# Block one's opening in a new order: the first half of features through modulation, then keys, filter layers and queries

## The chip, the cores and the metric

One core of one Trainium2 chip runs the whole program. The metric is device time in microseconds of one execution, the median of the runs shown. The engines are named as in the profile: PE is TensorE (PEld its weight loads), DVE is VectorE, ACT is ScalarE, POOL is GpSimd, SP is SyncE, which only issues DMAs here.

## What is computed

Two transformer blocks on 256 tokens of 1024 features. The change touches the start of the first one alone. Everything is float32. Cut to what matters:

```python
mx = (sc @ w_mod[l] + b_mod[l])[:, None, :]          # sc = silu(c)
mc = scc @ w_mod[l] + b_mod[l]                       # scc = silu(c_ctx)
sh1, sc1, g1, sh2, sc2, g2 = jnp.split(mx, 6, axis=-1)
csh1, csc1, cg1, csh2, csc2, cg2 = jnp.split(mc, 6, axis=-1)
hc = modulate(rms_norm(ctx, norm1_g[l]), csh1, csc1)  # h * (1 + scale) + shift
pkv = hc @ w_in[l][:, OFF_K:OFF_HY]                   # keys and values of the context
spec_x = hyena_spectrum(n_lat, hy_f_w1[l], ...)       # a small network with two sine layers
hx = modulate(rms_norm(x, norm1_g[l]), sh1, sc1)
yx, _, _ = mixer_sublayer(hx, kc, vc, rope, w_in[l], ...)   # queries, keys, values, hyena, fourier, gates
x = x + g1 * yx
h2 = modulate(rms_norm(x, norm2_g[l]), sh2, sc2)
x = x + g2 * expert_choice_moe(h2, w_router[l], w_gate[l], w_up[l], w_down[l])
```

Behind it come a final norm and a second block of two layers.

## The kernel before

Each engine has a program of its own, written out by hand in the order in which it runs; counting semaphores join them. `c.xtv`, `c.mod` and the like are such counters, `P.wait_ge(c.mod, 3)` a wait. Every engine executes strictly in its program's order, so a wait holds all that is written behind it.

Loads: the list `queue` is issued by SP in its order (L2867 to L2876). A 1 MB weight tile goes to one of six ring slots, and its DMA waits until the slot's last reader is done. `wmod` is the modulation weight. It has 12 column blocks of 512 columns, each in two loads (the two halves of the 1024 input features). `MODS` gives the order in which the blocks are done: `p` counts places in that order, `n` is the block. Blocks 0 and 1 are the two halves of the shift `sh1`, 2 and 3 those of the scale `sc1`.

One modulation block goes through four steps. `mod_products` on PE multiplies the two conditioning rows with eight weight slices (L506), `mod_evict` copies the sums out of PSUM on DVE or ACT, `mod_turn` on PE turns them into columns with four matmuls (L516), and `mod_add` on DVE adds the bias (L1436). `affA` is (1 + scale) times the norm's gain. Once scale and shift of a half are there, `turned_rows` on DVE and ACT apply them to the turned tokens of x (transposed on PE, L665) and write `XT1`. `high_half` (ACT) and `low_half` (DVE) then split `XT1` into `XTH` and `XTL`, two reduced-precision parts. The first weights are split the same way by `part()`: ACT writes the high part and DVE the low part (L1409). A product of split operands is three matmuls, `mm3` (L488 to L490). `q_half(m, h)` is such a product for the queries: tokens m (128 of them), half h of the features. `keys_values` (L641) multiplies the unsplit `XT1` (or `XT2`, the context) with the unsplit weight `wkv`; its argument `ks` lists the eight slices of 128 features.

The filter network: `filter_in(0)` and `filter_in(1)` are its two layers. A small matmul on PE is followed by a chain of seven DVE operations that reduce the sine's argument, and by ACT's sine. `filter_out` and `filter_sum` follow, `context_rows` turns the context's tokens. `turn_over(b, n)` issues n matmuls of the identity with itself into PSUM bank b; nobody reads them. After the queries and keys, `beside()` spreads the hyena, fourier and gate products between the steps of attention.

## Time and profile before

| what | us |
|---|---|
| median of 3 runs | 2299.32 |
| lowest and highest | 2298.85, 2299.82 |
| the profiled execution | 2296.84 |
| its span | 2295.5 |
| block one up to the first expert products | about 325 |
| expert stage | about 325 to 1219 |

The profiled execution is one run with the hardware profiler; its span is the time from the first to the last instruction. A timeline row is a run of equal instructions: start, busy time, engine, line, operation, written tile, read tiles, shape and count, and in brackets how long the engine had been idle and who ended that. A window row gives, for a stretch, the busy time of each engine, the clock that TensorE was granted (1.00 is full), the share of the 16 DMA engines and what they moved. The chain is followed back from the last instruction, so it names what everything waited for. A matmul of float32 appears as two records, a transpose as one.

### The profile page before, as it was taken

The numbers are of one execution on the slowest core, as the hardware profiler recorded it, in microseconds if no ns is written. First come the engines' busy times: TensorE is split into PE (matmuls) and PEld (weight loads), VectorE is DVE, ScalarE is ACT, GpSimd is POOL, SyncE is SP. The second block draws the span as 40 slices with busy tenths as digits, with TensorE's granted clock in tenths as the row PEclk, the third lists the DMA queues.
The fourth block names the chain that finished last, engine by engine and source line by source line (L and its number), as shares of the span: only waits on it lengthen the run. The fifth ranks groups of instructions, "written<-read, shape, count | busy, mean of one in ns | idle before, by whom it ended". The sixth has DMA issues, their size and how long they took to land.

```text
span 2295.5 us, 28914 instructions
## 1 busy us (share of the span) xinstructions
PE 1927.1 (84%) x12324; PEld 1348.0 (59%) x12324; DVE 982.9 (43%) x1219; ACT 668.9 (29%) x811; POOL 66.8 (3%) x144
## 2 busy tenths in 40 slices
PE   7899998556555566655589999999999999999998
PEld 4777962111111111111137998779998999778997
DVE  4745651000000000000006657875667666876656
ACT  4432420000000000000004444554445444455444
POOL 0000000000000000000001001010000000100000
PEclk9999999887878888787899999999999999999999
DMA  9156899999999999999997564245544555324552
GB/s 373 67 197 233 320 388 429 431 431 431 431 431 429 432 431 431 430 430 433 431 399 282 195 207 157 110 149 188 196 165 175 185 198 181 141 100 168 199 193 85
DMA packets 53489, 647.44 MB, mean 282 GB/s; under 512 B 5936, under 2 KB 6448, under 8 KB 10096
## 3 DMA queue, kind: packets, MB, share of 16 engines
q1 hardware_dynamic: 53360, 645.59, 70.5%
q8 instruction: 97, 1.59, 0.3%
q14 instruction: 32, 0.26, 0.0%
HBM read 644.52 MB, written 1.05 MB: 281 GB/s over the span
## 4 chain that ended last, share of the span: by engine, by line
PE 57%; DMA 32%; DVE 7%; ACT 2%; issue 1%; POOL 0%; SPq 0%; DVEq 0%; ACTq 0%; POOLq 0%
DMA wide_b<-in_experts 29%; PE PS L488 14%; PE PS L490 13%; PE PS L489 13%; PE PS L986 4%; PE PS L951 4%; DMA ring<-in_wgt 1%; DMA ahead<-in_wmod 1%; DVE low L1895 1%; PE PS L929 1%; DVE low L1409 1%; PE PS L641 1%; DVE PS L1920 1%; PE PS L1263 1%; DVE XR L1959 1%
## 5 line engine op out<-in xcount | busy, mean ns | idle before, releaser
L1895 DVE TENSOR_TENSOR low<-ring,WH 128x2048 fp32r<-128x2048 f32 (+1 forms) x163 | 372.1, 2283 | 182.5 <-ACT WH L2284 179.9
L488 PE MATMUL PS<-XH,WH 128*128 128x256 f32 x1408 | 396.9, 282 | 3.4 <-DVE XL L1927 3.3
L489 PE MATMUL PS<-XL,WH 128*128 128x256 f32 x1408 | 395.1, 281 | 0.0
L490 PE MATMUL PS<-XH,low 128*128 128x256 f32 x1408 | 393.1, 279 | 0.0
L2284 ACT ACTIVATE WH<-ring 128x2048 fp32r<-128x2048 f32 (+1 forms) x164 | 313.1, 1909 | 26.9 <-DMA ring<-in_fg 18.9
L488 PEld LDWEIGHTS PS<-XH,WH 128*128 128x128 f32 x1408 | 264.5, 188 | 7.0 <-issue 5.2
L490 PEld LDWEIGHTS PS<-XH,low 128*128 128x128 f32 x1408 | 267.5, 190 | 0.0
L489 PEld LDWEIGHTS PS<-XL,WH 128*128 128x128 f32 x1408 | 264.6, 188 | 1.4
L1877 DVE TENSOR_TENSOR T1S<-T1S,PS 128x512 f32<-128x512 f32 x16 | 11.0, 688 | 536.7 <-PE PS L951 536.7
L951 PE MATMUL PS<-ring,big 128*32 128x512 f32 x936 | 133.8, 721 | 57.9 <-DMA ring<-in_experts 57.9
L2558 ACT ACTIVATE T1S<-PS 128x512 f32<-128x512 f32 x16 | 9.6, 597 | 540.2 <-PE PS L951 540.2
L986 PE MATMUL PS<-wide_b,PBT 128*32 128x512 f32 x480 | 86.6, 886 | 75.2 <-DMA wide_b<-in_experts 75.2
L951 PE MATMUL PS<-wide_a,big 128*32 128x512 f32 x480 | 81.1, 827 | 71.4 <-DMA wide_a<-in_experts 71.3
L488 PE MATMUL PS<-WH,FH 128*128 128x512 f32 x352 | 139.6, 397 | 0.4 <-DVE FL L2025 0.4
L490 PE MATMUL PS<-WH,FL 128*128 128x512 f32 x352 | 138.5, 393 | 0.0
L489 PE MATMUL PS<-low,FH 128*128 128x512 f32 x352 | 138.4, 393 | 0.0
L1885 DVE TENSOR_TENSOR T1S<-PS,ATG 128x512 f32<-128x512 f32 x32 | 22.1, 692 | 262.4 <-PE PS L986 261.8
L951 PE MATMUL PS<-wide_b,big 128*32 128x512 f32 x480 | 77.0, 790 | 56.3 <-DMA wide_b<-in_experts 56.3
L951 PEld LDWEIGHTS PS<-ring,big 128*32 128x32 f32 x936 | 31.9, 128 | 154.6 <-issue 80.7
L488 PE MATMUL PS<-WH,XH 128*128 128x512 f32 (+1 forms) x256 | 104.6, 408 | 4.5 <-DVE low L1895 3.5
L986 PEld LDWEIGHTS PS<-wide_b,PBT 128*32 128x32 f32 x480 | 19.1, 154 | 140.2 <-DMA wide_b<-in_experts 85.8
L490 PE MATMUL PS<-WH,XL 128*128 128x512 f32 (+1 forms) x256 | 99.5, 388 | 0.0
(447 smaller groups left out, 2816.1 us busy)
## 6 DMA issues: line engine op xcount, KB each, us to landing
wide_b<-in_experts SPq DMA_DIRECT2D x30, 4096.0 KB, 23.7
wide_a<-in_experts SPq DMA_DIRECT2D x29, 4096.0 KB, 23.8
ring<-in_experts SPq DMA_DIRECT2D x28, 4096.0 KB, 24.0
ring<-in_fg SPq DMA_DIRECT2D x44, 1024.0 KB, 5.0
ring<-in_fu SPq DMA_DIRECT2D x44, 1024.0 KB, 5.0
ring<-in_fd SPq DMA_DIRECT2D x44, 1024.0 KB, 4.9
ring<-in_wmod SPq DMA_DIRECT2D x22, 1024.0 KB, 5.8
ring<-in_wgt SPq DMA_DIRECT2D x12, 1024.0 KB, 9.2
```

The lines of the kernel that those rows point to most:

```text
L488: t.matmul(o, l[0], r[0], start=start, stop=False, skip_group_check=True)
L489: t.matmul(o, l[0], r[1], start=False, stop=False, skip_group_check=True)
L490: return t.matmul(o, l[1], r[0], start=False, stop=stop, skip_group_check=True)
L641: x = t.matmul(PS[:, 4 + half, m * 256:m * 256 + 256], src[:, k, m * 128:m * 128 + 128], w.ap[:, k, :], start=k == 0, stop=k == 7, skip_gr ...
L929: x = t.matmul(PS[:, bank, at:at + 32 * (e1 - e0)], XN[:, m, k * 128:k * 128 + 128], big[:, m * 512 + 32 * e0:m * 512 + 32 * e1], start=m ...
L951: x = t.matmul(PS[32 * j:32 * j + 32, b, :], (XG0[:, k, ex * 32:ex * 32 + 32] if ex < 2 else XG2[:, k, ex * 32 - 64:ex * 32 - 32]), w.ap[: ...
L986: x = t.matmul(PS[32 * j:32 * j + 32, n, :], PT[:, 0, i * 128 + 32 * j:i * 128 + 32 * j + 32], ws[j // 2].ap[:, j % 2, n * 512:n * 512 + 5 ...
L1263: x = t.matmul(PS[:, o + m, h * 64:h * 64 + 64], PT2[:, b, i * w + kt * 128:i * w + kt * 128 + 128], v, start=kt == 0, stop=kt == w // 128 ...
L1409: own(v.tensor_tensor(low[:, w.slot.index, s], w.flat[:, s], low[:, 4 + parted % 2, s].bitcast(f32), ALU.subtract).then_inc(*c.wl.up()), c.wl)
L1895: own(v.tensor_tensor(low[:, w.slot.index, 0:size], w.flat, WH[:, w.slot.index, 0:size].bitcast(f32), ALU.subtract).then_inc(*c.wl.up()), ...
L1920: own(v.tensor_tensor(x, x, g[:, 4 * j:4 * j + 4].unsqueeze(2).to_broadcast([128, 4, 128]), ALU.mult).then_inc(*c.rg.up()), c.rg)
L2284: return a.activation(o, i, ACT.Copy)
```

## The change

The order of modulation blocks becomes (2, 0, 3, 1), so scale and shift of the first half of features come first. The loads of base (identity and small tables) and x go ahead of the modulation weights, `wkv` goes behind the first four of them, the filter constants behind that. On PE six identity matmuls open the program. The transposes of x come behind the first product, `keys_values` of x is cut in two halves by features, the first one ahead of the queries, and the filter layers go behind it. `mod_products(3)` is cut in two and laid between the query products. Block p = 2 is now evicted by DVE, not ACT. `affA` is made in two halves (`first_affine`). Identity matmuls are put at four more places. DVE does x's norm ahead of the first eviction.

```diff
-MODS = (2, 3, 0, 1, 4, 5, 6, 7, 8, 9, 10, 11)
+MODS = (2, 0, 3, 1, 4, 5, 6, 7, 8, 9, 10, 11)
...
-                                 w.ap[:, k, :], start=k == 0, stop=k == 7, skip_group_check=True)
+                                 w.ap[:, k, :], start=k == 0 and (m == 0 or half == 1), stop=k == 7, skip_group_check=True)
...
+            turn_over(6, 6)
             mod_products(0)
-            mod_turn(0)
-            filter_in(0)
-            mod_products(1)
             for m in range(2):
...
+            mod_turn(0)
+            mod_products(1, [0])
+            turn_over(6, 4)
+            mod_products(1, [1])
+            turn_over(6, 2)
             mod_turn(1)
-            filter_in(1)
+            turn_over(6, 5)
+            for m in range(2):
+                keys_values(0, XT1, m, range(4))
+            filter_in(0)
             mod_products(2)
             mod_turn(2)
-            mod_products(3)
+            filter_in(1)
 
 
             q_half(0, 0)
+            mod_products(3, [0])
+            q_half(1, 0)
+            mod_products(3, [1])
             mod_turn(3)
-            q_half(1, 0)
             filter_out(0)
+            for m in range(2):
+                keys_values(0, XT1, m, range(4, 8))
             q_half(0, 1)
             filter_out(1)
             q_half(1, 1)
@@ -687,12 +697,10 @@
             context_rows(0)
             context_rows(1)
             filter_out(2)
-            keys_values(0, XT1, 0, range(8))
             filter_sum(1)
             context_rows(2)
             context_rows(3)
             filter_out(3)
-            keys_values(0, XT1, 1, range(8))
             filter_sum(2)
...
+            V.wait_ge(*l_x)
+            own(rsqrt(0, 2).then_inc(*c.rs.up()), c.rs)
+            own(v.tensor_scalar(XN[:, 0, :], XR[:, 0, :], stat[:, 0:1], None, ALU.mult).then_inc(*c.xn.up()), c.xn)
             mod_evict(0)
             V.wait_ge(*l_id)
             mod_add(0)
...
+            first_affine(0)
+            mod_add(1)
+            turned_rows(0)
+            low_half(0)
             filter_in(0)
...
+            mod_evict(2)
+            mod_add(2)
+            first_affine(1)
+            part()
             filter_in(1)
...
+            mod_add(3)
+            turned_rows(1)
             low_half(1)
             part()
```

The loads, at the head of SP's queue. Before:

```order
L2872 DMA filters<-in_c2T 128x256 [waits barrier_Pool_Activation_PE_DVE_SP_release]
L2876 DMA ring<-in_wmod 128x2048 x2
L2872 DMA base<-in_base 128x253
L2872 DMA XR<-in_x_t 128x2048
L2872 DMA filters<-in_filt 64x1408
L2876 DMA ring<-in_wmod 128x2048 x4
```

Now:

```order
L2886 DMA filters<-in_c2T 128x256 [waits barrier_Pool_Activation_PE_DVE_SP_release]
L2886 DMA base<-in_base 128x253
L2886 DMA XR<-in_x_t 128x2048
L2890 DMA ring<-in_wmod 128x2048 x4
L2890 DMA HRI<-in_wkv 128x2048
L2886 DMA filters<-in_filt 64x1408
L2890 DMA ring<-in_wmod 128x2048 x2
```

base, x and wkv have moved ahead, the filter constants back, and the modulation loads stand behind base and x.

PE from the second turned block to the first query product (L516 is mod_turn, L506 mod_products, L570 filter_in, L641 keys_values, L485 turn_over). Before:

```order
L516 MATMUL PS<-base,ATG 128x2 [waits s_modev]
L516 MATMUL PS<-base,ATG 128x2 x3
L570 MATMUL PS<-big,filters 64x256 [waits s_fa,s_fv]
L506 MATMUL PS<-ring,c2s 32x512 [waits s_ring4,s_mod]
L506 MATMUL PS<-ring,c2s 32x512 x3
L506 MATMUL PS<-ring,c2s 32x512 [waits s_ring5]
L506 MATMUL PS<-ring,c2s 32x512 x3
L516 MATMUL PS<-base,ATG 128x2 [waits s_modev]
L516 MATMUL PS<-base,ATG 128x2 x3
L506 MATMUL PS<-ahead,c2s 32x512 [waits s_wide1,s_mod]
L506 MATMUL PS<-ahead,c2s 32x512 x3
```

Now:

```order
L516 MATMUL PS<-base,ATG 128x2 x3
L485 MATMUL PS<-base 128x128 x5
L641 MATMUL PS<-HRI,ATG 128x256 [waits s_xtv,s_wide4]
L641 MATMUL PS<-HRI,ATG 128x256
L641 MATMUL PS<-HRI,ATG 128x256 [waits s_xta]
L641 MATMUL PS<-HRI,ATG 128x256 x5
L570 MATMUL PS<-filters 64x256 [waits s_l_filt]
L506 MATMUL PS<-ring,c2s 32x512 [waits s_ring4,s_mod]
L506 MATMUL PS<-ring,c2s 32x512 x3
L506 MATMUL PS<-ring,c2s 32x512 [waits s_ring5]
L506 MATMUL PS<-ring,c2s 32x512 x3
```

The first key products stand ahead of both filter layers and of the third block's product; the fourth block's product (from ahead) is no longer here.

DVE from the split of the first half to that of the first query weight (L1556 and L1569 are low_half, L1409 and L1417 part, L1436 and L1444 mod_add). Before:

```order
L1436 TENSOR_TENSOR modT<-PS,base 128x8 [waits s_modtr,s_fv]
L1373 TENSOR_SCALAR ATG<-PS,affA,modT 128x256 [waits s_xtp,s_mod]
L1373 TENSOR_SCALAR ATG<-PS,affA,modT 128x256 [waits s_vec]
L1556 TENSOR_TENSOR XTL<-ATG,XTH 128x1024 [waits s_xta,s_xtv]
L1409 TENSOR_TENSOR low<-ring,low 128x1024 [waits s_wh,s_xtv]
L1409 TENSOR_TENSOR low<-ring,low 128x1024 [waits s_wh,s_wl]
```

Now:

```order
L1569 TENSOR_TENSOR XTL<-ATG,XTH 128x1024 [waits s_xta,s_xtv]
L1473 TENSOR_SCALAR big<-PS,base 64x256 [waits s_flt,s_xtv]
L1402 TENSOR_SCALAR big<-big 64x256 [waits s_vec]
L1403 TENSOR_SCALAR big<-big 64x256 [waits s_vec]
L1405 SCALAR_TENSOR_TENSOR big<-big 64x256 [waits s_vec] x3
L1406 TENSOR_SCALAR big<-big 64x256 [waits s_vec]
L1437 COPY ATG<-PS 128x512 [waits s_modmm,s_fv]
L1444 TENSOR_TENSOR modT<-PS,base 128x8 [waits s_modtr,s_modev]
L1555 TENSOR_SCALAR affA<-modT 128x4x2 [waits s_mod]
L1556 TENSOR_TENSOR affA<-affA,base 128x4x2 [waits s_vec]
L1417 TENSOR_TENSOR low<-ring,low 128x1024 [waits s_wh,s_a1]
L1417 TENSOR_TENSOR low<-ring,low 128x1024 [waits s_wh,s_wl]
```

The first filter layer, the copy of the third block out of PSUM, its bias and the second half of affA now lie between the two splits.

## Rows read from the trace of the kernel before

**Rows 1.** Page, part 4: the chain that ended last, by line

```profile
DMA wide_b<-in_experts 29%; PE PS L488 14%; PE PS L490 13%; PE PS L489 13%; PE PS L986 4%; PE PS L951 4%; DMA ring<-in_wgt 1%; DMA ahead<-in_wmod 1%; DVE low L1895 1%; PE PS L929 1%; DVE low L1409 1%; PE PS L641 1%; DVE PS L1920 1%; PE PS L1263 1%; DVE XR L1959 1%
```


**Rows 2.** Windows; columns: stretch, length, busy us of each engine, PEclk, DMA, GB/s

```profile
110.00:130.00 20.00, 19.86 (x122) 14.98 (x121) 10.42 (x14) 7.62 (x14) 0.00 (x0) 1.00 0.19 66
...
400.00:500.00 100.00, 59.17 (x356) 15.77 (x348) 5.53 (x8) 1.96 (x4) 1.18 (x4) 0.86 1.00 431
```


**Rows 3.** Timeline of PE, the opening; columns: start us, busy us

```profile
6.74 1.93 PE L506 MATMUL PS<-ring,c2s 128*32 128x512 f32 x8 [6.74 <-DMA ring<-in_wmod]
9.20 1.94 PE L506 MATMUL PS<-ring,c2s 128*32 128x512 f32 x8 [0.53 <-DMA ring<-in_wmod]
...
16.89 1.94 PE L506 MATMUL PS<-ring,c2s 128*32 128x512 f32 x8 [1.23 <-DMA ring<-in_wmod]
...
21.15 2.09 PE L665 MATMUL PS<-base,XN 128*128 128x128 f32 x16
23.07 0.95 PE L516 MATMUL PS<-base,ATG 128*128 128x2 f32 x8
...
24.53 1.92 PE L506 MATMUL PS<-ring,c2s 128*32 128x512 f32 x16
...
29.34 1.06 PE L506 MATMUL PS<-ahead,c2s 128*32 128x512 f32 x8 [1.07 <-DMA ahead<-in_wmod]
31.74 1.93 PE L506 MATMUL PS<-ahead,c2s 128*32 128x512 f32 x8 [1.33 <-DMA ahead<-in_wmod]
```


**Rows 4.** Timeline of PE, second query half, first key product, wait at 81.85

```profile
43.49 0.47 PE L488 MATMUL PS<-low,XTH 128*128 128x512 f32 x1 [1.41 <-DVE low L1409]
...
46.41 1.12 PE L577 MATMUL PS<-filters,big 64*128 64x512 f32 x2
...
53.23 3.72 PE L641 MATMUL PS<-HRI,ATG 128*128 128x256 f32 x16
...
81.85 0.36 PE L488 MATMUL PS<-XTH,low 128*128 128x256 f32 x1 [3.31 <-DVE low L1409]
```


**Rows 5.** Timeline of ACT (first row) and POOL (second row), inside attention's start

```profile
72.09 0.60 ACT L2445 ACTIVATE T1S<-PS 128x512 f32<-128x512 f32 x1 [8.67 <-PE PS L641]
...
55.81 2.91 POOL L2813 TENSOR_TENSOR stat<-stat,mhalf 128x16 f32<-128x16 f32 x1
```


**Rows 6.** Timeline of DVE from the first context rows to the keys' squares

```profile
58.35 1.12 DVE L1373 TENSOR_SCALAR XT<-PS,affA,modT 128x256 f32<-128x256 f32 x2 [3.00 <-PE PS L652]
...
61.42 0.18 DVE L1378 TENSOR_TENSOR stat<-stat 128x16 f32<-128x16 f32 x1
...
67.50 2.48 DVE L1409 TENSOR_TENSOR low<-ring,low 128x1024 fp32r<-128x1024 f32 x2
72.80 0.69 DVE L1615 TENSOR_REDUCE stat<-T1S 128x8 f32<-128x512 f32 x1 [2.82 <-ACT T1S L2445]
```


**Rows 7.** Timeline of ACT in the opening: first square of x, a PSUM copy

```profile
12.91 1.06 ACT L2287 ACTIVATE T1S<-XR 128x1024 f32<-128x1024 f32 x1 [9.76 <-DMA XR<-in_x_t]
...
26.57 0.60 ACT L2284 ACTIVATE ATG<-PS 128x512 f32<-128x512 f32 x1 [4.17 <-PE PS L506]
```


**Rows 8.** Timeline of DVE in the opening: filter layer, affine, last bias add

```profile
18.11 0.53 DVE L1465 TENSOR_SCALAR big<-PS,base 64x256 f32<-64x256 f32 x1
...
20.66 0.28 DVE L1398 TENSOR_SCALAR big<-big 64x256 f32<-64x256 f32 x1
...
28.58 1.12 DVE L1373 TENSOR_SCALAR ATG<-PS,affA,modT 128x256 f32<-128x256 f32 x2
...
38.25 0.17 DVE L1436 TENSOR_TENSOR modT<-PS,base 128x8 f32<-128x8 f32 x1 [3.44 <-PE PS L516]
```


**Rows 9.** Windows, columns as in rows 2: stretches with low and high clock

```profile
82.00:86.00 4.00, 4.00 (x23) 4.00 (x24) 3.75 (x8) 0.00 (x0) 0.00 (x0) 0.61 0.18 74
...
31.80:35.00 3.20, 3.17 (x11) 1.27 (x12) 2.95 (x3) 1.91 (x3) 0.00 (x0) 0.50 1.04 417
35.00:38.00 3.00, 3.00 (x18) 2.52 (x18) 0.00 (x0) 0.00 (x0) 0.00 (x0) 0.98 1.01 418
```

More of the change, by code:

```diff
@@ L341, in program @@
         const(c2T[:, :, :], "c2T", l_c2T)
-        load_mod(0)
         const(base[:, :], "base", l_id)
         const(XR[:, :, :], "x_t", l_x)
+        load_mod(0)
+        load_mod(1)
+        load("wkv", 0, c.kv, 4, [Slot(HRI[:, :, :, :].rearrange("p a b c -> p (a b c)"), c.wide4)])
         const(filt[:, :], "filt", l_filt)
-        load_mod(1)
         load_mod(2)
@@ L353, in program @@
         const(ctx_t, "ctx_t", l_ctx)
-        load("wkv", 0, c.kv, 4, [Slot(HRI[:, :, :, :].rearrange("p a b c -> p (a b c)"), c.wide4)])
         const(cd[:, :, :], "cd", l_hyc)
@@ L501, in mod_products @@
                 P.wait_ge(c.c2s, 1)
-                for kh in range(2):
+                for kh in halves:
                     w = W["wmod", 2 * n + kh]
@@ L1542, in drain, with first_affine, turned_rows @@
                     pass
-            def turned_rows(p):
-                b = 2 * (p - 2)
-                mod_add(p)
+            def first_affine(h):
+                k = slice(4 * h, 4 * h + 4)
+                own(v.tensor_scalar(affA[:, k, 0:2], modT[:, 8 + 4 * h:12 + 4 * h, :], 1.0, None, ALU.add))
+                own(v.tensor_tensor(affA[:, k, 0:2], affA[:, k, 0:2], n1T[:, k].unsqueeze(2).to_broadcast([128, 4, 2]),
+                                    ALU.mult).then_inc(*c.a1.up()), c.a1)
+            def turned_rows(h):
+                b = 2 * h
                 V.wait_ge(c.xtp, 5 + b)
```

38 lines of the change are left out of this document (13 added, 25 removed).

## The prediction

> **What bounds the kernel now.** I read the page's chain by line first: its largest entry is the DMA of expert weights [rows 1]. The windows then separate the stages. In the expert stage TensorE works 59.17 of 100 us while the DMA queues move 431 GB/s; in attention (110 to 130 us) TensorE works 19.86 of 20 us at 66 GB/s [rows 2]. The expert loads start as block one frees its buffers, so an offset at the end of block one should pass through the expert stage nearly whole, and the question is how large an offset the beginning hands on.
>
> The beginning has three parts. Until about 31.8 us the modulation products wait for their loads: the starts at 6.74, 9.20, 29.34 and 31.74 are released by DMAs [rows 3]. Then TensorE does both query products of the first half of features, and waits again until 43.49 for the split query weights of the second half [rows 4]. From there to the last key product it has no gap. ScalarE sat idle for 8.67 us and squares the finished keys at 72.09; VectorE starts to reduce them at 72.80 [rows 5, 6]. From 72.80 on the order of work is the same in both kernels: reduction, reciprocal, key rotation, split of a weight, TensorE at 81.85 [rows 4]. So I work out when that reduction starts in the changed kernel. Call the start of q_half(0, 1) Q: Q is 43.49 before, and the reduction is Q + 29.31.
>
> **The loads.** One MB of weights lands 2.46 us after another (9.20 - 6.74), and x landed at about 12.9, where ScalarE starts on it [rows 3, 7]. In the new order base (0.13 MB) and x are ahead of the first modulation load. x, the first MB now, lands at about 6.7 + 0.5 = 7.2. Further MBs come at 9.65 and 12.1 (block 2, scale), 14.6 and 17.0 (block 0, shift), wkv 19.5; the filter constants (0.36 MB) at about 21.1; 23.5 and 26.0 (block 3), wq0 28.5, and block 1 at 31.0 and 33.4. The last modulation load comes about 1.7 us later than its 31.74. XN was ready 5.2 us after x landed (18.11 - 12.9) [rows 7, 8], so now at 12.4, ahead of need. From the context rows on the sum of bytes is as before, and nothing there is late.
>
> **First half of features.** The second half of block 2's product runs from 12.1 to 14.0 (1.94 us for eight records) [rows 3]. The sixteen transposes of x follow. They took 2.09 us at 21.15, at the high level of the clock; the products of 6.74 to 19.29 took 1.93 us for eight records where 24.53 has sixteen in 1.92, so TensorE ran at half speed (1.2 of 2.4 GHz) until about 21 us, although the granted clock's column is not lowered there [rows 3]. In the new order TensorE works without a gap from 12.1 on. I let the level rise about one third of the way into the transposes: they cost 2.9 us, between 2.0 and 3.9, and end at 16.9. Then: turn 0.95 [rows 3], bias add and handover 0.35, half a product 0.97 (half of 1.92), four matmuls of turn_over 0.5, half a product 0.97, all to 20.65; ScalarE's copy out of PSUM with handovers 0.75 [rows 7], turn 1.0: VectorE adds block 0's bias at 22.5. The two affine operations take 1.12 [rows 8]; the keys' first half starts at 24.0, with wkv long landed. Sixteen records of it took 3.72 us for eight k; half of each m is the same amount, so 3.65, to 27.65.
>
> Behind them on TensorE stands the first filter layer (I allow 0.65 for its small matmul), and behind that on VectorE the eviction of block 3, which the change moves to that engine. VectorE needs 2.83 us for a filter layer (18.11 to 20.94) [rows 8]. So: filter matmul to 28.3, layer 28.4 to 31.2, copy 0.7 to 31.95, turn to 33.05, add and affA 0.6 to 33.7, half a weight split 1.24 (half of 2.48) [rows 6], and q_half(0, 0) starts at 35.1. It started at 33.70 before, straight behind the product of 31.74 [rows 3]. The new place of the filter layer thus puts its 2.83 us on the path to the queries; before it lay beside the loads. The second layer goes behind the split and is free: 36.2 to 39.0, its sine done at 39.5, and its next reader comes at 44 or later.
>
> **Second half.** q_half took 2.92 us (43.49 to 46.41) [rows 4]. Now q_half, half a product, q_half, half a product: 2.95 + 0.97 + 2.95 + 0.97 = 7.85; copy out and handovers 0.75, turn 1.05: the last bias add comes 9.65 after q_half(0, 0) begins, at full clock. Before it, from 30.1 to 35.0, TensorE has only 1.6 us of thin work. In the row from 31.80 to 35.00 the level is 0.50 after similar idling, and after the idle 3.31 us at 78.55 the row 82 to 86 shows 0.61 [rows 9]. A low stretch there costs half its length, 1.6 us; I take 1.4. Sum: 35.1 + 9.65 + 1.4 = 46.15, against 38.25 before: 7.9 us later [rows 8]. The steps from that add to Q (affine, high half, low half, split) are the same, 5.24 us; filter_out and the keys' second half (1.1 + 3.65 = 4.75) fit just inside them, where TensorE had idled 1.41 [rows 4]. Q becomes 51.4.
>
> **From Q on** the two key products of x (2 x 3.65 = 7.3 us) are gone. By TensorE alone the last key product ends at Q + 28.5 - 7.3 = Q + 21.2, and the reduction could start at Q + 22.0. VectorE is in the way. It lost mainly waits: it had idled 3.00 us before 58.35 behind the first key product [rows 6]. Its row 58.35 (Q + 14.86) can now start at Q + 11.9, behind the reduction of the queries' squares; filter_out and the gains end at Q + 14.65. The inverse root comes from GpSimd, whose 2.91 us [rows 5] with handovers end 3.37 after that reduction, at Q + 15.25. From 61.42 to the split at 67.50 it is 6.08 us of dependent work, then 2.48 of split, and the keys' reduction stands behind it [rows 6]: Q + 15.3 + 6.05 + 2.5 = Q + 23.85. That is 5.45 less than 29.31, not 7.3.
>
> **Sum:** +7.9 - 5.45 = +2.45 us, I take +2.4. The profiled execution took 2296.84 us (span 2295.5); with the change 2299.2. The median of the runs shown is 2299.32, 2.5 above the profiled one, so the prediction is 2301.7. The seventeen added matmuls (about 2 us) cost little by themselves: six run while TensorE waits for its first load, five in the gap before the keys, and six (0.7 us) lie in the path above.
>
> **A rule to weigh.** The idle stretches above lower TensorE's level in rows [rows 9]. The Trainium skill, page "Perfetto Trace Analysis", section "Matmul Optimizations", says that the engine scales with its use and that matmuls should run back to back. This trace agrees; the added matmuls stand in the first half alone, and by the rule the thin stretch before q_half stays uncovered.
>
> **Rivals.** *The clock decides, and against it.* Before, the level stayed low through about 14 us of broken work from 6.74 on [rows 3]. If it stays low from 12.1 until the keys start, my sum grows by 1.0 (transposes), 0.95 (first turn), 2.0 (both half products), 0.6 (turn_over) and 0.95 (second turn): +5.5, so +7.9 us, 2307.2. It passes the bound once the rise comes some 4 us later than I take it, behind the first turn. For it: that earlier stretch. Against: work from 12.1 on has no gap, and of the gapless work begun at 31.74 the row to 35.00 shows 0.50 and the next one 0.98 [rows 9]. The Trainium skill, page "TensorE: Matmul & The Clock Gate", section "Part 4: PE-mode transpose", says that transposes do not count as busy for the clock. No row here tells, for the transposes of 21.15 were already fast.
>
> *The clock helps.* The rise comes before the transposes (-0.9), the stretch before q_half stays high (-1.4) and the low one after 81.85 is not met (-1.6): +2.4 - 3.9 = -1.5, 2297.8. For it: the turn_over matmuls. Against: the waits that lower it are all still there.
>
> *VectorE is no bound.* If TensorE's own work sets the reduction (Q + 22.0), the gain is 7.3 instead of 5.45, and the sum is +0.6, 2299.9. Against it stand 6.08 + 2.48 us of VectorE work ahead of the reduction in program order [rows 6]. With both helps -3.3, 2296.0, which is still within 0.2%.
>
> *A gain over 0.2%.* It would need Q at or before 44.3 although q_half(0, 0) starts later than it did: the filter layer would have to take no time on VectorE, and the clock would have to help too. I have no rows for it.
>
> **Numbers.** 0.2% of 2299 is 4.6 us, about what a measurement of this kernel can tell from no change. Forecast (+0.5 to +4.5): 0.55. VectorE no bound or clock helps (-3.5 to +0.5): 0.24. Clock against it: 0.15, of which most is over 4.6. Gain over 4.6: 0.06. The range leaves out the gain and the worst of the clock: 2296.3 to 2306.5. Faster 0.06, same 0.79, slower 0.15.
>
> **What would show it.** The profile of the changed kernel should have: x's squares on ScalarE from about 7.2 us; the transposes at about 14; the first key product at about 24 and q_half(0, 0) at about 35; the last bias add of the beginning at about 46 and Q at about 51; no key product of x between the two context stages; VectorE working without a gap before it reduces the keys' squares at 75.2; everything behind that shifted by one constant of 2.4. A first key product at 29 or later speaks for the clock's rival. If the reduction follows ScalarE's square directly, VectorE was no bound. If the offset at 81.85 is not the offset at 340 us, the claim that it passes through is wrong.

## Result: 5 us slower, and the profile after

The changed kernel took 2303.61 us in the median of 19 runs (2298.72 to 2305.94), the kernel before 2298.65 in 19 runs taken beside them (2294.24 to 2302.32). The ratio is 1.002, with a 95% interval of 1.0014 to 1.0026, so 3.2 to 6.0 us slower; the medians stand 4.96 apart. The forecast was 2301.7, or 2.4 us slower than before, in a range of 2296.3 to 2306.5. The time lies in the range, the direction was right, and the loss is about twice the size forecast.

The profiled execution took 2304.29 us (span 2303.0). Most executions lie within 4 us of their kernel's median, a few up to 7 (one of the kernel before took 2305.17 where the median of its group was 2297.96), so a step is read from the place in the trace where it happens, and not from the end of the span.

The chain of the changed kernel by line, page, part 4, has the same entries ahead as [rows 1]; the DMA of the expert weights still leads:

```profile
DMA wide_b<-in_experts 29%; PE PS L488 14%; PE PS L490 13%; PE PS L489 13%; PE PS L959 4%; PE PS L994 4%; DVE low L1910 1%; DMA ring<-in_wgt 1%; DVE PS L1935 1%; PE PS L506 1%; PE PS L937 1%; PE PS L861 1%; DVE XR L1974 1%; PE PS L1271 1%; PE PS L767 0%
```

PE of the changed kernel, timeline (columns as in rows 3 and 4). The landings come first: 9.57 and 11.96 stand against 9.65 and 12.1 in the forecast.

```profile
9.57 1.93 PE L506 MATMUL PS<-ring,c2s 128*32 128x512 f32 x8 [3.29 <-DMA ring<-in_wmod]
11.96 1.93 PE L506 MATMUL PS<-ring,c2s 128*32 128x512 f32 x8 [0.46 <-DMA ring<-in_wmod]
13.82 2.74 PE L663 MATMUL PS<-base,XN 128*128 128x128 f32 x16
16.40 0.95 PE L516 MATMUL PS<-base,ATG 128*128 128x2 f32 x8
...
18.70 1.16 PE L485 MATMUL PS<-base 128*128 128x128 f32 x8
...
24.27 3.69 PE L641 MATMUL PS<-HRI,ATG 128*128 128x256 f32 x16 [0.36 <-DVE ATG L1381]
27.89 0.64 PE L570 MATMUL PS<-filters 33*64 33x256 f32 x2
28.46 1.92 PE L506 MATMUL PS<-ring,c2s 128*32 128x512 f32 x16
32.27 1.67 PE L516 MATMUL PS<-base,ATG 128*128 128x2 f32 x8 [1.89 <-DVE ATG L1437]
33.87 1.11 PE L570 MATMUL PS<-big,filters 64*64 64x256 f32 x2
36.03 0.77 PE L488 MATMUL PS<-low,XTH 128*128 128x512 f32 x1 [1.05 <-DVE low L1417]
...
48.83 5.41 PE L641 MATMUL PS<-HRI,ATG 128*128 128x256 f32 x16
53.88 0.58 PE L488 MATMUL PS<-low,XTH 128*128 128x512 f32 x1
```

Up to the first key product all went as forecast (24.27 against 24.0). Then TensorE waits 1.89 us for VectorE's copy (L1437) and 1.05 us for its split (L1417). The same kinds of work took different times. Four matmuls of a turn took 0.95 us at 16.40 and 1.67 at 32.27; half the keys of x took 3.69 at 24.27 and 5.41 at 48.83. The granted clock explains it. The windows of the changed kernel (columns as in rows 2; the clock is the third number from the end):

```profile
32.00:34.00 2.00, 1.73 (x9) 1.71 (x10) 0.22 (x1) 1.94 (x3) 0.00 (x0) 0.63 1.06 442
34.00:36.00 2.00, 0.98 (x2) 0.16 (x3) 1.82 (x5) 0.18 (x1) 0.00 (x0) 0.50 0.97 401
36.00:38.00 2.00, 1.97 (x5) 1.63 (x6) 1.93 (x3) 0.00 (x0) 0.00 (x0) 0.50 1.02 414
38.00:40.00 2.00, 2.00 (x8) 1.59 (x7) 1.83 (x6) 0.00 (x0) 0.00 (x0) 0.66 1.00 407
...
50.00:52.00 2.00, 2.00 (x6) 1.64 (x5) 1.83 (x2) 1.94 (x3) 0.00 (x0) 0.50 0.96 397
52.00:54.00 2.00, 2.00 (x9) 1.63 (x8) 1.93 (x3) 1.94 (x4) 0.00 (x0) 0.75 0.55 201
```

TensorE was at its lower level (0.50, 1.2 GHz) from about 32.5 to 39.3, and again from about 49.6 to 53. In the kernel before only 31.8 to 35 of this stretch was low [rows 9]; its windows from 38 to 54 all read 1.00.

VectorE of the changed kernel, from the first filter layer to the end of the stretch:

```profile
28.64 0.54 DVE L1473 TENSOR_SCALAR big<-PS,base 64x256 f32<-64x256 f32 x1 [1.93 <-PE PS L570]
...
31.52 0.69 DVE L1437 COPY ATG<-PS 128x512 f32<-128x512 f32 x1
34.05 0.17 DVE L1444 TENSOR_TENSOR modT<-PS,base 128x8 f32<-128x8 f32 x1 [1.83 <-PE PS L516]
...
34.65 2.48 DVE L1417 TENSOR_TENSOR low<-ring,low 128x1024 fp32r<-128x1024 f32 x2
...
47.45 0.17 DVE L1444 TENSOR_TENSOR modT<-PS,base 128x8 f32<-128x8 f32 x1 [7.42 <-PE PS L516]
...
69.35 0.17 DVE L1386 TENSOR_TENSOR stat<-stat 128x16 f32<-128x16 f32 x1 [0.73 <-POOL stat L2827]
...
75.42 2.49 DVE L1417 TENSOR_TENSOR low<-ring,low 128x1024 fp32r<-128x1024 f32 x2
77.94 0.69 DVE L1630 TENSOR_REDUCE stat<-T1S 128x8 f32<-128x512 f32 x1
```

The filter layer stands between the keys and the copy, as the prediction put it. The last bias add of the beginning is at 47.45 (forecast 46.15). At the end VectorE has no idle time ahead of its reduction at 77.94; ScalarE had finished the square long before:

```profile
75.72 0.60 ACT L2459 ACTIVATE T1S<-PS 128x512 f32<-128x512 f32 x1 [5.06 <-PE PS L641]
```

The wait of [rows 4] at 81.85 is now at 86.99 on PE:

```profile
86.99 0.42 PE L488 MATMUL PS<-XTH,low 128*128 128x256 f32 x1 [3.42 <-DVE low L1417]
```

It comes 5.14 us later, and the end of the program in the medians 4.96.

### The profile page after: what moved, and what is told of

Its sections match the earlier page's. It is cut to its first block, busy times and chain, and to the rows that moved or that the text cites. A ratio compares the mean times of both kernels' runs of the same rounds, so it can differ in the third digit from the quotient of the medians.

```text
span 2303.0 us, 28986 instructions
## 1 busy us (share of the span) xinstructions
PE 1948.6 (85%) x12358; PEld 1359.1 (59%) x12358; DVE 983.7 (43%) x1222; ACT 668.4 (29%) x810; POOL 67.0 (3%) x144
## 3 DMA queue, kind: packets, MB, share of 16 engines
HBM read 644.52 MB, written 1.05 MB: 280 GB/s over the span
## 4 chain that ended last, share of the span: by engine, by line
PE 58%; DMA 31%; DVE 7%; ACT 2%; issue 1%; POOL 1%; SPq 0%; DVEq 0%; ACTq 0%; POOLq 0%
DMA wide_b<-in_experts 29%; PE PS L488 14%; PE PS L490 13%; PE PS L489 13%; PE PS L959 4%; PE PS L994 4%; DVE low L1910 1%; DMA ring<-in_wgt 1%; DVE PS L1935 1%; PE PS L506 1%; PE PS L937 1%; PE PS L861 1%; DVE XR L1974 1%; PE PS L1271 1%; PE PS L767 0%
## 5 line engine op out<-in xcount | busy, mean ns | idle before, releaser
L959 PE MATMUL PS<-wide_a,big 128*32 128x512 f32 x480 | 86.0, 871 | 74.6 <-DMA wide_a<-in_experts 74.6
L959 PE MATMUL PS<-wide_b,big 128*32 128x512 f32 x480 | 82.4, 840 | 50.9 <-DMA wide_b<-in_experts 50.9
L489 PE MATMUL PS<-low,XH 128*128 128x512 f32 (+1 forms) x256 | 99.4, 388 | 0.0
```

The lines of the kernel that those rows point to most:

```text
L489: t.matmul(o, l[0], r[1], start=False, stop=False, skip_group_check=True)
L959: x = t.matmul(PS[32 * j:32 * j + 32, b, :], (XG0[:, k, ex * 32:ex * 32 + 32] if ex < 2 else XG2[:, k, ex * 32 - 64:ex * 32 - 32]), w.ap[: ...
```

## Experiments

In the tables below "Q" is the start of q_half(0, 1), "keys" the first key product of x, "reduction" VectorE's reduction of the keys' squares, "wait" the start on PE that was 81.85, and "340" the first load into wide_b of the expert stage, at 340.10 before. All from the profiled execution. Two kernels were timed in one run each. The last column is the median with the ratio to the runs of before that were taken beside it.

| kernel | keys | q_half(0, 0) | Q | reduction | wait | 340 | median, ratio [95%] |
|---|---|---|---|---|---|---|---|
| before | | 33.70 | 43.49 | 72.80 | 81.85 | 340.10 | 2298.65 |
| after | 24.27 | 36.03 | 53.88 | 77.94 | 86.99 | 346.71 | 2303.61, 1.0020 [1.0014, 1.0026] |
| filter behind | 23.20 | 32.86 | 51.62 | 75.66 | 84.71 | 342.24 | 2301.91, 1.0020 [1.0010, 1.0030] |
| more turn_overs | 23.69 | 34.84 | 50.05 | 73.95 | 83.01 | 340.79 | 2300.86, 1.0018 [1.0009, 1.0027] |
| both | 24.88 | 34.45 | 50.49 | 74.40 | 83.45 | 340.54 | 2300.79, 1.0013 [1.0003, 1.0022] |
| no query rotation | 24.48 | 36.07 | 54.10 | 76.64 | 85.69 | 343.65 | 2301.30, one run |
| no turn_overs | 22.55 | 36.45 | 54.11 | 78.08 | 87.13 | 348.41 | 2304.66, 1.0024 [1.0015, 1.0034] |
| combined | 24.15 | 33.72 | 50.90 | 73.88 | 82.93 | 343.70 | 2299.89, 1.0003 [0.9994, 1.0012] |
| combined, third fill | 23.82 | 33.39 | 49.56 | 72.54 | 81.59 | 339.92 | 2297.76, 0.9995 [0.9986, 1.0005] |
| before + turn_overs | | 33.85 | 43.04 | 72.38 | 81.44 | 339.00 | 2295.97, 0.9994 [0.9984, 1.0004] |
| before + fewer | | 33.53 | 42.69 | 73.57 | 82.62 | 339.48 | 2297.74, 0.9996 [0.9987, 1.0006] |
| before + new loads | | 38.78 | 49.50 | 80.36 | 89.41 | 346.25 | 2305.93, one run |

There is one profile of each kernel, and its clock is partly chance. Seven of these kernels (after, filter behind, more turn_overs, both, no query rotation and the two combined ones) have the same program up to the first key product. Their transposes took 1.97 to 3.61 us, and that product started at 23.20 to 24.88. So the absolute times of two kernels can differ by more than a microsecond before any edit does its work, and below the spans from the first key product on are compared.

**The filter layers behind the copy and the split.** On PE filter_in(0) goes behind the third block's product and filter_in(1) behind q_half(1, 0); on DVE and ACT both go behind the weight's split.

```diff
-            filter_in(0)
             mod_products(2)
+            filter_in(0)
             mod_turn(2)
-            filter_in(1)
...
             q_half(1, 0)
+            filter_in(1)
             mod_products(3, [1])
```

> The changed kernel with the first filter layer taken out of the way of block 3: on VectorE the copy of block 3 out of PSUM, its bias add, the second half of affA and the split of the first query weight stand ahead of the filter layers; on TensorE block 3's product stands ahead of the first filter matmul and the second filter matmul behind q_half(1, 0). Theory of the path (the 2.83 us filter layer on VectorE delays the queries): q_half(0, 0) starts at about 34.2 instead of 36.03, the last bias add of the beginning comes about 1.3 us earlier (one filter matmul of 0.6 is added to the path), the keys' reduction about 1.3 us earlier than 77.94, and the time is about 3.5 us above the kernel before instead of 5. Theory of the clock (the offset is low-clock time and nothing else): the stretch of 0.50 moves along with the queries, and the reduction gains less than 0.5 us.

The first key product itself came 1.07 us earlier here (23.20). From it to q_half(0, 0) it takes 9.66 us instead of 11.76, to the reduction 52.46 instead of 53.67. The edit thus takes 2.10 us out at q_half(0, 0), of which 1.21 are left at the reduction. The 2.10 are not the layer alone: the turn of the third block ran at the full level here (29.72, 1.05 us instead of 1.67), where TensorE waited 0.31 us ahead of it and not 1.89. The rest of the gain is lost in the second half: filter_in(1) now stands between the two halves of the fourth block's product, and filter_out waits for its sine:

```profile
45.54 1.09 PE L577 MATMUL PS<-filters,big 64*128 64x512 f32 x2 [0.76 <-ACT big L2395]
46.56 5.41 PE L641 MATMUL PS<-HRI,ATG 128*128 128x256 f32 x16
```

The keys' second half still runs at the lower level. The median is not told apart from that of the changed kernel.

**More matmuls of the identity in the waits.** Seven ahead of the turn of the third block, five ahead of q_half(0, 0), three ahead of the last turn.

```diff
             mod_products(2)
+            turn_over(5, 7)
             mod_turn(2)
             filter_in(1)
+            turn_over(5, 5)
...
             mod_products(3, [1])
+            turn_over(5, 3)
             mod_turn(3)
```

> The changed kernel with 15 more identity matmuls into the free PSUM bank 5, in TensorE's waits: seven behind block 3's product, five behind the second filter matmul, three ahead of the last turn. Nothing else is moved. Theory of the clock: the level stays at 1.00 from 30 us to Q; the second turn takes 0.95 instead of 1.67, q_half(0, 0) 2.95 instead of 4.5, the keys' second half 3.65 instead of 5.41; Q comes about 3.2 us earlier than 53.88, the reduction too, and the time is about 1.8 us above the kernel before. Theory of the path: the low clock is only a companion of waits for VectorE, the matmuls that it slows are waited for anyway, and Q gains less than 1 us.

PE of this kernel, the turn and the keys' second half:

```profile
31.70 1.05 PE L516 MATMUL PS<-base,ATG 128*128 128x2 f32 x8
...
46.11 3.72 PE L641 MATMUL PS<-HRI,ATG 128*128 128x256 f32 x16
```

A window of it (columns as in rows 2), where the changed kernel had 0.50:

```profile
36.00:38.00 2.00, 2.00 (x13) 1.32 (x15) 1.86 (x5) 0.00 (x0) 0.00 (x0) 1.00 1.04 422
```

The turn is back at 1.05 and the keys' half at 3.72; no window shows a lowered clock before 82 us. From the first key product to the reduction it takes 50.26 us instead of 53.67. Only matmuls that nobody reads were added. Of these 3.41 us, 3.25 lie ahead of Q, where the lower level ran: 0.61 in the turn, 1.54 in q_half(0, 0), 1.10 in the keys' half. The last 0.16 lie behind Q, where neither kernel shows a lowered clock, and are unexplained. The medians do not show the gain: 1.0018 [1.0009, 1.0027] is not told apart from 1.0020 [1.0014, 1.0026]. The Trainium skill, page "Perfetto Trace Analysis", section "Matmul Optimizations", says that the matmul engine scales with its use, so that matmuls should run back to back; this pair of traces agrees (3.25 us up to Q for 15 added matmuls).

**Both edits together**, with the matmuls at the fitting places (one and seven around the turn of the third block).

```diff
-            filter_in(0)
             mod_products(2)
+            filter_in(0)
+            turn_over(5, 1)
             mod_turn(2)
-            filter_in(1)
+            turn_over(5, 7)
...
             q_half(1, 0)
+            filter_in(1)
             mod_products(3, [1])
+            turn_over(5, 3)
             mod_turn(3)
```

> Both edits together (the filter layers behind, identity matmuls in the three waits). If both causes are on the path and add up, Q comes 4.5 to 5 us earlier than 53.88, and the time equals that of the kernel before within 1 us. If they cover each other (the low clock fills the same time as the wait for VectorE), the sum is that of the larger alone, about 3.2.

From keys to reduction it takes 49.52 us, 4.15 less than in the changed kernel, where 4.5 to 5 were expected: the two gains add up nearly (1.21 + 3.41 = 4.62). The four kernels together show how they overlap (us from the first key product):

| kernel | to q_half(0, 0) | to Q | to the reduction |
|---|---|---|---|
| after | 11.76 | 29.61 | 53.67 |
| filter behind | 9.66 | 28.42 | 52.46 |
| more turn_overs | 11.15 | 26.36 | 50.26 |
| both | 9.57 | 25.61 | 49.52 |

With the clock held up, the filter layer's place costs 1.58 us at q_half(0, 0) (11.15 - 9.57) and 0.74 at the reduction. Without the added matmuls it is 2.10 and 1.21: the 0.5 us between the two are low clock that goes with the layer's place. Counted from the changed kernel's first key product, the reduction would be at 73.79, still 0.99 behind the 72.80 of before: the two edits account for 4.15 of the 5.14 us. The first key product of this kernel came 0.6 us later, which hides a part of the gain in the absolute times.

**VectorE as the bound.** The rotation of the queries (four DVE operations, L1426 to L1429) is left out, and one small operation stands in its place; the queries are thus unrotated.

```diff
-            own(rope(QK, RQ, 8).then_inc(*c.qn.up()), c.qn)
+            own(v.tensor_tensor(T2[:, 0:64], QK[:, 0, 0, :], QK[:, 0, 1, :], ALU.add).then_inc(*c.qn.up()), c.qn)
```

> The changed kernel without the rotation of the queries on VectorE (four operations, 3.9 us, replaced by one small one), so part of the computation is left out. Theory that VectorE bounds the keys' reduction: VectorE's own work would bring it 3.7 us forward, but the last key product and ScalarE's square stop it at about Q + 22.4, so it starts about 1.6 us earlier relative to Q (24.06 before the edit). If TensorE were the bound already, the distance stays 24.06.

VectorE's split and reduction in this kernel:

```profile
71.92 2.49 DVE L1417 TENSOR_TENSOR low<-ring,low 128x1024 fp32r<-128x1024 f32 x2
76.64 0.69 DVE L1630 TENSOR_REDUCE stat<-T1S 128x8 f32<-128x512 f32 x1 [2.24 <-ACT T1S L2459]
```

The reduction comes at Q + 22.54 instead of Q + 24.06, and now it does wait, 2.24 us, for ScalarE's square and so for the last key product. That is TensorE's own limit, which the prediction had put at Q + 22.0. VectorE's queue is what took 1.5 us of the gain from the moved keys; this step stands. Up to Q this kernel is the changed kernel once more, and from the first key product to Q it took 29.62 us against 29.61, with the lower level in the same three places (turn 1.50, keys' half 5.41).

**All that is wanted of the changed order at once.** The combined kernel has both edits, the gains and filter_out(2) moved out of VectorE's chain between the root of the queries' norm and the keys' reduction, and twelve identity matmuls in the wait at 82 us.

```diff
             for q in range(2, 4):
                 quarter("why", 0, 7, q)
+            turn_over(1, 12)
...
             filter_out(0)
+            V.wait_ge(*l_gain)
+            gained(RQ, q_gain)
+            gained(RK, k_gain)
             filter_out(1)
...
-            V.wait_ge(*l_gain)
-            gained(RQ, q_gain)
             context_rows(0)
-            filter_out(2)
             V.wait_ge(c.hsq, 1)
             own(v.tensor_reduce(stat[:, 0:16], T1[:, :].rearrange("p (h d) -> p h d", h=16), X,
                                 ALU.add).then_inc(*c.red.up()), c.red)
+            filter_out(2)
             context_rows(2)
             filter_out(3)
-            gained(RK, k_gain)
```

> The kernel of both edits (filter layers behind, more identity matmuls), and two more: on VectorE the gains of the rotation tables are made in the wait behind filter_out(0) and the queries' squares are reduced ahead of filter_out(2), and twelve identity matmuls stand ahead of the products of why1. If VectorE and the GpSimd root behind it bound the keys' reduction, it comes 1.1 us closer to Q (23.9 to 22.8); with Q at about 50 the reduction comes at 72.8 to 73.4, as before the change, and the time lies 0 to 2 us below the kernel before by the high clock after 82 us. If TensorE is the bound, the distance to Q stays 23.9.

Its reduction comes at Q + 22.98, 1.08 earlier against Q than in the changed kernel, about what the two edits had left. But the lower level came back in one place. PE of the combined kernel:

```profile
44.82 1.09 PE L577 MATMUL PS<-filters,big 64*128 64x512 f32 x2 [0.75 <-ACT big L2399]
45.84 5.41 PE L641 MATMUL PS<-HRI,ATG 128*128 128x256 f32 x16
```

And its window (columns as in rows 2):

```profile
46.00:48.00 2.00, 2.00 (x6) 1.53 (x7) 0.89 (x1) 1.97 (x2) 0.00 (x0) 0.52 1.04 434
```

The kernel with both edits has the same wait of 0.75 us in front of the same matmul and took 3.72 for the keys. TensorE's program is the same in both up to there. So after a wait of this kind the level fell in one execution and not in the other.

**A third fill.** The combined kernel with six more identity matmuls in that wait.

```diff
             mod_turn(3)
+            turn_over(5, 6)
             filter_out(0)
```

> The combined variant with six more identity matmuls behind the turn of the fourth block, where TensorE waited 0.75 us for the sine ahead of filter_out, and behind which the keys' second half had run at the low clock (5.41 us). Theory (a short piece of idling there decides the level): the keys' second half takes 3.7 us, Q at 49.4 to 50.0 instead of 50.90, the reduction at 72.4 to 73.0 instead of 73.88, and a time 1 to 1.5 us under the combined variant, so within 1 us of the kernel before. Rival (the level in this stretch was scatter between executions of alike programs, since the third variant with the same matmuls had none of it): the keys' second half may take either length, and the fill itself then costs up to 0.7 us of the path where its matmuls outlast the wait.

PE of this kernel, the same place:

```profile
45.14 1.12 PE L577 MATMUL PS<-filters,big 64*128 64x512 f32 x2
46.19 3.72 PE L641 MATMUL PS<-HRI,ATG 128*128 128x256 f32 x16
```

There is no wait and no window with a lowered clock up to 92 us, Q is at 49.56 and the reduction at 72.54, all within what the first theory expected. That the level is safe here, and was not lucky in one execution, one profile can't show. The time is that of the kernel before (0.9995 [0.9986, 1.0005]), and its wait on PE ends at 81.59 against 81.85. The intervals of the two combined kernels do not overlap that of the changed one (1.0014 to 1.0026), so the gain of all the edits together shows in the medians too. The new order can thus be brought back to where the old one was, but not ahead of it in any way that these runs can measure.

**The added matmuls taken out.** The changed kernel without its seventeen identity matmuls in the opening.

```diff
-            turn_over(6, 6)
             mod_products(0)
...
             mod_products(1, [0])
-            turn_over(6, 4)
             mod_products(1, [1])
-            turn_over(6, 2)
             mod_turn(1)
-            turn_over(6, 5)
```

> The changed kernel without its seventeen identity matmuls. Theory that they raise the clock early (a): the transposes, the turns and the products up to 22 us run at the low level in part, and the keys start at 24.5 to 26 us (24.27 with them) although 1.45 us of matmuls are gone from the path. Theory that the clock rises in any case behind the gapless work from 12 us on (b): the keys start at about 22.9, and Q comes 1.4 us earlier.

PE of this kernel, the transposes and the first key product:

```profile
13.78 2.29 PE L662 MATMUL PS<-base,XN 128*128 128x128 f32 x16
...
22.55 6.45 PE L641 MATMUL PS<-HRI,ATG 128*128 128x256 f32 x16 [1.58 <-DVE ATG L1377]
```

A window of it (columns as in rows 2):

```profile
24.00:26.00 2.00, 2.00 (x6) 1.62 (x5) 0.99 (x1) 0.00 (x0) 0.00 (x0) 0.50 0.98 410
```

The keys start 1.72 us earlier, but at the lower level, and take 2.76 us longer (6.45 instead of 3.69), so they end 1.04 later. Q is 54.11 against 53.88, but the way there differs. Here the turn of the third block was fast (1.05 for 1.67), q_half(0, 0) with its handover was slow throughout (5.39 from its start to the next product, for 4.47), and the keys' second half was fast:

```profile
50.17 3.72 PE L641 MATMUL PS<-HRI,ATG 128*128 128x256 f32 x16
54.11 0.47 PE L488 MATMUL PS<-low,XTH 128*128 128x512 f32 x1 [0.22 <-DVE low L1413]
```

So the near equality at Q comes from levels that fell differently in two executions, and what the seventeen matmuls are worth in all stays open; the medians don't tell the two kernels apart. Over the eight kernels of the new order q_half(0, 0) is clear: to the next product it took 4.47, 4.50, 4.63 and 5.39 us in the four without identity matmuls between the keys and it, and 2.92 to 2.96 in the four with them. The keys' second half is not: 5.41 in three of the first four and 3.72 here, 3.72 in three of the second four and 5.41 in the combined one. In the changed kernel four of the added matmuls start at 18.70 and the next product at 19.79: 1.09 us, so 0.27 each at full clock and not the 0.12 of my sum.

**The waits of the kernel before filled.** Matmuls around the turn of the third block (three, four), five between the halves of the fourth block's product, and twelve in the wait at 82.

```diff
             mod_products(2)
+            turn_over(5, 3)
             mod_turn(2)
-            mod_products(3)
+            turn_over(5, 4)
+            mod_products(3, [0])
+            turn_over(5, 5)
+            mod_products(3, [1])
...
                 quarter("why", 0, 7, q)
+            turn_over(1, 12)
```

> The kernel before with identity matmuls alone added, in TensorE's waits: three behind block 0's product, four behind its turn, five between the two halves of block 1's product (bank 5), and twelve ahead of the products of why1 (bank 1), where TensorE waited 3.31 us at 81.85. Theory that low clock costs what its stretches say: the stretch from 31.8 to 35 goes (0.9 on block 1's product, 0.7 on q_half), Q comes 1.6 us earlier than 43.49, the reduction 1.6 earlier than 72.80, and the stretch from 82.9 to 86.3 goes too, another 1.6; the time is about 3.2 us below the kernel before. Theory that the low stretches lie beside other waits: Q gains under 0.5 and the whole under 1 us.

PE of this kernel, where the fourth block's product ends:

```profile
31.55 1.38 PE L485 MATMUL PS<-base 128*128 128x128 f32 x10
32.86 1.07 PE L506 MATMUL PS<-ahead,c2s 128*32 128x512 f32 x8
33.85 0.50 PE L488 MATMUL PS<-low,XTH 128*128 128x512 f32 x1
```

The loads of the two halves, in this kernel (from the view of tile ahead):

```profile
L2881 SPq DMA_DIRECT2D ahead<-in_wmod x2: 433/434/434, 8.6 to 9.1; - x2
DMA to landing us min/median/max: 21.8/22.8/23.7
```

The second one is issued at 9.07 and lands 23.7 us later, at 32.8; in the kernel before it landed at 31.7. So the five matmuls end within 0.1 us of the landing, and the product starts at 32.86. The clock was full: from the landing to q_half(0, 0) it takes 1.1 us where it took 2.0 before, and from there to Q 9.19 instead of 9.79. That is some 1.5 us, near the 1.6 that the first theory gave to this place. But the load came 1.1 us later in this execution, so that q_half(0, 0) started at 33.85 against 33.70 and only 0.45 showed at Q. Whether the edit or chance made the load late stays open. The twelve matmuls at 82 us gave another 1.55 (from the wait to the transposes at L728 5.73 us, before 7.28). At 340 us 1.1 of it all was left; the median is 2.0 lower, which the interval does not tell from nothing.

**The same with the five taken out again.**

```diff
             turn_over(5, 4)
             mod_products(3, [0])
-            turn_over(5, 5)
             mod_products(3, [1])
```

> The kernel before with identity matmuls at three places: three ahead of the turn of the third block and four behind it, and twelve ahead of the product of why (in the wait at 81.85); none between the two halves of the fourth block's product, where five of them had held the second half of the product 1.1 us back. Theory (the low clock behind broken work is what these buy, and only the five were in the way): no granted clock under 0.9 between 28 and 100 us, q_half(0, 0) at 32.7 to 33.7, Q (43.49 before) at 41.9 to 42.4, the reduction of the keys at 71.1 to 71.7 (72.80 before), the wbr load and wide_b 2 to 2.7 us earlier than before (242.03, 340.10), and a time 2 to 3 us under the kernel before. Rival (loads set the start of the fourth block's second half at 31.7, and a low clock comes back between 28 and 36, since the five kept TensorE at work there): Q at 43.0 to 43.5 and a time as before within 1 us.

The reason given there, that the five had held the product 1.1 us back, does not stand: the load had landed that much later. This kernel's second load landed at 32.04.

VectorE's reduction in this kernel:

```profile
73.57 0.69 DVE L1619 TENSOR_REDUCE stat<-T1S 128x8 f32<-128x512 f32 x1 [2.83 <-ACT T1S L2449]
```

And one of its windows (columns as in rows 2):

```profile
44.00:46.00 2.00, 2.00 (x6) 1.60 (x5) 0.53 (x1) 1.13 (x3) 1.11 (x4) 0.50 1.02 422
```

Both theories missed. The level was low from about 29.7 to 33.1, as the rival had it, and q_half(0, 0) started at 33.53, 1.5 us behind the landing (1.1 with the five matmuls, 2.0 before). Q came at 42.69, 0.8 earlier than before. But then the level was low from about 43.3 to 46.8, behind the same wait of 1.4 us at Q that had left it alone in the kernel before, and the reduction came 0.77 later than there. It is the second place where the same wait went either way.

**The new loads under the old order.** The kernel before with base and x ahead of the modulation weights and wkv ahead of the filter constants.

```diff
-        load_mod(0)
         const(base[:, :], "base", l_id)
         const(XR[:, :, :], "x_t", l_x)
-        const(filt[:, :], "filt", l_filt)
+        load_mod(0)
         load_mod(1)
+        load("wkv", 0, c.kv, 4, [Slot(HRI[:, :, :, :].rearrange("p a b c -> p (a b c)"), c.wide4)])
+        const(filt[:, :], "filt", l_filt)
...
-        load("wkv", 0, c.kv, 4, [Slot(HRI[:, :, :, :].rearrange("p a b c -> p (a b c)"), c.wide4)])
```

> The kernel before with the new order of its loads alone: base and x ahead, wkv behind the fourth modulation load, filter constants behind it. The order of work on the engines is the old one, so TensorE waits at its first filter matmul until the constants land at about 21 us. The last modulation load comes 1.7 to 2.4 us later than 31.74, the clock is as before, and Q and the keys' reduction come about 2 us later (45.5 and 74.8). If wkv costs nothing in its new place, both stay.

PE of this kernel (a single run, 2305.93 us):

```profile
21.78 1.11 PE L570 MATMUL PS<-filters 33*64 33x256 f32 x2 [5.06 <-DMA filters<-in_filt]
22.82 3.60 PE L506 MATMUL PS<-ring,c2s 128*32 128x512 f32 x16
```

I had expected some 2 us and got 7.56 at the wait (89.41 for 81.85). The filter layer still stood early in PE's program, waited 5.06 us for constants that now came late, and held the next product behind it, at the lower level by its duration (3.60 instead of 1.92). Q came at 49.50, 6.01 later, and q_half(0, 1) behind it ran partly at the lower level (windows of 0.53 and 0.61 from 50 to 54). The two parts of the change need each other: with the filter layers in their old place the new loads cost 7.56 us at the wait. In their new place the layers cost 1.2 of the changed kernel's 5.1.

## Point by point

- **The loads: right.** 9.57 and 11.96 for 9.65 and 12.1; x's squares on ScalarE at 7.03 for 7.2; wkv was there in time.
- **The rise of the clock during the transposes: right.** They took 2.74 us (2.9 forecast), and the turn behind them 0.95. That 2.74 lies so near 2.9 is luck: in the seven kernels with this opening they took 1.97 to 3.61, about the whole range of the prediction (2.0 to 3.9), and the turn took 0.95 in each. The rival of a level that stays low until the keys is out. Without any identity matmul ahead of it the rise came within the same scatter (2.29 us, then 0.95). The Trainium skill, page "TensorE: Matmul & The Clock Gate", section "Part 4: PE-mode transpose", would have transposes not count as busy; here the level rose while sixteen of them ran, with a product of 1.93 us directly ahead, so the rule does not show in these rows, nor do they refute it.
- **keys at 24.0: right** (24.27). Two misses cancelled here. From the turn behind the transposes to the keys it takes 7.87 us for 7.1 in the sum, since the six matmuls in the path cost 0.27 us each and not 0.12; and that turn started at 16.40 for 16.9. The added matmuls do not "cost little by themselves".
- **The filter layer on the path: right in place, less in size.** The prediction put its 2.83 us on the path to the queries. Moving it away gives back 2.10 at q_half(0, 0), of which 1.58 with the clock held up, and at the reduction 1.21 and 0.74.
- **The clock ahead of the queries: the step that was mis-sized.** "A low stretch there costs half its length, 1.6 us; I take 1.4." In q_half(0, 0) itself that was right: 1.54. The term was too small because the low clock was in two more places, 3.25 us up to Q in all. It began in the turn of the third block (1.67 for 1.05) and so put off the bias add (34.05 for about 33.1), and it came back in the keys' half (next point). q_half(0, 0) came at 36.03 for 35.1, the last bias add at 47.45 for 46.15.
- **"The steps from that add to Q are the same, 5.24 us": wrong.** They took 6.43. filter_out and the keys' half "fit just inside them" only at full clock; at the lower level the half took 5.41 for 3.65, and TensorE itself set Q. In the kernels more turn_overs and no turn_overs, where this half took 3.72, the steps took 5.32 us and TensorE waited 0.22 for VectorE: there the cover held. With so little slack (4.75 of 5.24 us), the cover's own risk belonged in the sum.
- **Q to the reduction: right.** Q + 24.06 for Q + 23.85, by VectorE's queue, as shown by its missing idle time and by the kernel without the rotation.
- **The rivals.** Neither a clock that helps nor a VectorE that is no bound came true; there is no gain over 0.2%. What came was the forecast's own mechanism with more low clock in it.
- **Sum.** The excess over the forecast is 77.94 - 75.2 = 2.74: 0.27 at the keys, 0.66 to q_half(0, 0), 0.37 to the bias add, 1.19 to Q, 0.21 to the reduction (0.04 is rounding). Of low clock there were 3.25 us up to Q, where the forecast had 1.4: 1.85 of the 2.7 are the clock. The rest, 0.85, are small errors of the same sign, which I can't divide further.
- **The offset passes through: not as "one constant".** It is 5.14 at the wait, 6.61 at the first wide_b load, and 4.96 in the medians. By the prediction's own sign (the same offset at 81.85 and at 340) the claim fails in this execution, though the medians end near the first number. Up to the issue at 226.75 (221.66 before) the offset is still 5.09. The weight tile (wgt) issued there landed after 12.1 us and not 10.6, and TensorE waited 2.65 us instead of 1.12 for ScalarE, in whose program the split of this tile stands ahead. The later load of wbr is then issued at 248.62 for 242.03, +6.59. Over the eleven kernels beside the one before, the offset changed between the two places by -1.4 to +3.0 us, so the 1.5 here is no more than the scatter. These are the issues on SP, before and then after:

```profile
242.03 17.29 SPq L2876 DMA_DIRECT2D ring<-in_wbr  x4
340.10 0.33 SPq L2876 DMA_DIRECT2D wide_b<-in_experts  x1
```

```profile
248.62 17.29 SPq L2890 DMA_DIRECT2D ring<-in_wbr  x4
346.71 0.33 SPq L2890 DMA_DIRECT2D wide_b<-in_experts  x1
```

What stays open is why that tile landed later, and whether it does so in every run.

## What to carry to other kernels

When thin work is put between two waits of TensorE, price what runs behind it at the lower clock too, and everything that was hidden with less slack than that: a cover of 4.75 us under 5.24 was no cover at 1.2 GHz. A moved operation is paid on the engine whose queue it joins: the filter layer's small matmul cost TensorE little, while its chain on VectorE held the copy that the queries waited for. Matmuls that nobody reads took 3.25 us of low clock out of one stretch and some 1.5 out of another, but neither shows in a median by itself. Before a filler is blamed for a late start, look up when the load landed: here the load was 1.1 us late in that execution, and the five matmuls ended with it. And one profile is one draw of the clock: compare spans from a common point, and look for the same stretch in several kernels.

## What was not expected of the hardware

- After equal waits the granted level went either way. Behind 0.75 us of idle at about 45 the keys' half took 3.72 us in one kernel and 5.41 in another with the same TensorE program there; behind 1.4 us at Q the level stayed at 1.00 in the kernel before and in "before + turn_overs" and fell to 0.50 in "before + fewer" and to 0.53 in "before + new loads". The Trainium skill, page "TensorE: Matmul & The Clock Gate", section "Part 1: The HAM clock gate (the "warmup" mystery)", says that the count of slow matmuls differs from run to run of one kernel; these traces agree. The seven kernels with one opening, with transposes of 1.97 to 3.61 us, are the nearest to that.
- A wait of 3.4 us on PE at 83 us did not always lower it: with both edits PE waited 3.41 us and the next windows show 1.00, with more turn_overs alone it waited 3.43 and the row from 82 to 86 shows 0.57. Of the eight kernels with a wait of 3.3 to 3.4 us there, three took 5.7 us from it to the next transposes (both, no query rotation, before + new loads) and five 7.1 to 8.4. The kernel before and the changed one are both among the five (7.28 and 7.27), so this does not enter their difference.
- A float32 matmul of the 128x128 identity (two records) takes 0.27 us at the full level and 0.49 at the lower one (six in 2.93 us at the program's start; the granted clock's column reads 1.00 there, and the level is read from the durations).
